# Hybrid encoder layer on one core: value products of the neighbourhood attention with the values as stationary operand, two heads on the two halves of the output partitions

## What is computed

```python
# tokens lie on a grid 64 columns wide; a query row sees 8 key rows, a block of 16 query columns sees 32 key columns
s = einsum('bhnqd,bhrnkd->bhnqrk', q_b, k_blk) + bias      # masked 2-D relative bias
p = softmax(s over the 8 x 32 keys)
o = einsum('bhnqrk,bhrnkd->bhnqd', p, v_blk)               # the value products
na = o * silu(ga)
y = x + gate * (concat(na, retention) @ w_out)
```

## Time and profile before

| | us |
|---|---|
| median of 3 runs | 3115.77 |
| profiled execution, its own time | 3119.01 |
| its span | 3117.2 |
| TensorE busy in the span | 3063.3 (98%) |
| VectorE, ScalarE, GpSimd busy | 1459.4, 862.3, 577.2 |

### The profile page before, as it was taken

The page is one execution under the profiler, slowest core; times in us unless marked ns, Lnnn a source line. Parts: engine busy times, 40 slices in busy tenths (PEclk is TensorE's granted clock), DMA queues, the critical chain, the costliest instruction groups (busy, mean ns, idle before and its releaser), DMA issues.

```text
span 3117.2 us, 49473 instructions
## 1 busy us (share of the span) xinstructions
PE 3063.3 (98%) x16480; PEld 2600.1 (83%) x16480; DVE 1459.4 (47%) x3181; ACT 862.3 (28%) x1832; POOL 577.2 (19%) x633
## 2 busy tenths in 40 slices
PE   7999999999999999999999999999999999999999
PEld 3888888888886888888888888889999988888887
DVE  4334333343334433333333333335666666777775
ACT  3232232222322211111111111125675672111111
POOL 1111111111111540000000000002333332333331
PEclk9999999999999999999999999999999999999999
DMA  7444445444446842122222212248688665555553
GB/s 281 151 143 160 147 138 167 141 137 159 144 145 250 303 136 78 72 83 80 82 77 83 83 70 79 80 154 238 185 258 251 208 202 184 202 202 202 202 202 142
DMA packets 208757, 491.04 MB, mean 158 GB/s; under 512 B 23275, under 2 KB 85739, under 8 KB 204165
## 3 DMA queue, kind: packets, MB, share of 16 engines
q1 hardware_dynamic: 199255, 462.64, 44.6%
q0 software_dynamic: 9424, 27.43, 2.7%
HBM read 306.83 MB, written 191.00 MB: 160 GB/s over the span
## 4 chain that ended last, share of the span: by engine, by line
PE 64%; issue 1%; ACT 1%; DVE 1%; DMA 1%; SPq 0%; POOL 0%; ACTq 0%; DVEq 0%
PE proj L329 27%; PE t_bank L1761 7%; PE o_bank L1512 7%; PE s_bank L1761 4%; PE o_bank L1761 4%; PE t_bank L1498 3%; PE s_bank L1488 3%; PE r_kv L1068 2%; PE s_bank L1751 1%; PE r_so L1078 1%; PE r_so L1077 1%; PE r_so L1055 1%; PE s_bank L1743 1%; PE r_qkT L1047 1%; DMA bias_table<-tables_d 1%
## 5 line engine op out<-in xcount | busy, mean ns | idle before, releaser
L329 PE MATMUL proj<-w_att_hi,a_h_hi 128*128 128x512 f32 x2560 | 1024.3, 400 | 13.1 <-DVE a_h_lo L430 7.1
L329 PE MATMUL proj<-w_att_hi,a_h_lo 128*128 128x512 f32 x2560 | 1001.9, 391 | 0.0
L329 PE MATMUL proj<-w_att_lo,a_h_hi 128*128 128x512 f32 x2560 | 1000.2, 391 | 0.0
L329 PEld LDWEIGHTS proj<-w_att_hi,a_h_hi 128*128 128x128 f32 x2560 | 483.2, 189 | 106.9 <-DVE a_h_lo L430 7.4
L329 PEld LDWEIGHTS proj<-w_att_hi,a_h_lo 128*128 128x128 f32 x2560 | 482.0, 188 | 102.9
L329 PEld LDWEIGHTS proj<-w_att_lo,a_h_hi 128*128 128x128 f32 x2560 | 483.4, 189 | 92.5
L1512 PE MATMUL o_bank<-v_strip,probs_T 120*128 120x64 f32 (+2 forms) x2112 | 278.9, 273 | 12.8 <-ACT probs_T L1353 11.1
L1512 PEld LDWEIGHTS o_bank<-v_strip,probs_T 120*128 120x128 f32 (+2 forms) x2112 | 266.3, 193 | 27.3 <-ACT probs_T L1353 16.0
L1307 POOL CAST q_block<-q_strip 128x512 fp32r<-128x512 f32 x80 | 49.6, 620 | 1270.0 <-DMA q_strip<-q_d 950.5
L1345 ACT ACTIVATE probs<-biased,neg_max 128x360 f32<-128x360 f32 (+3 forms) x320 | 218.4, 684 | 90.8 <-DVE neg_max L1400 87.9
L561 POOL TENSOR_TENSOR qk_stat<-qk_stat,minus_half 128x8 f32<-128x8 f32 x80 | 131.3, 1642 | 526.0 <-DVE qk_stat L655 526.0
(11 more groups left out here) (155 smaller groups left out, 4260.0 us busy)
## 6 DMA issues: line engine op xcount, KB each, us to landing
k_strip<-kT_d SPq DMA_DIRECT2D x12, 1920.0 KB, 11.3
a_x<-in_x SPq DMA_DIRECT2D x40, 512.0 KB, 4.4
a_xT<-in_xT SPq DMA_DIRECT2D x40, 512.0 KB, 5.2
h_d<-a_h_hi SPq DMA_DIRECT2D x40, 512.0 KB, 2.7
h_d<-a_h_lo SPq DMA_DIRECT2D x40, 512.0 KB, 3.5
kT_d<-k_parts SPq DMA_DIRECT2D x80, 256.0 KB, 3.5
q_strip<-q_d SPq DMA_DIRECT2D x40, 512.0 KB, 6.7
o_x<-in_x SPq DMA_DIRECT2D x40, 512.0 KB, 4.4
```

The lines of the kernel that those rows point to most:

```text
L329: last = self.nc.tensor.matmul(bank, h[:, par, k, :], w[:, n, k, :], start=(k == 0 and j == 0), stop=(k == KB - 1 and j == 2))
```

## The change

The value products swap operands. The values [keys x 64] of a head are stationary, the turned probabilities [keys x 128 queries] moving, and the result is transposed, [64 x 128 queries]. Heads 0 and 2 write output partitions 0 to 63, heads 1 and 3 partitions 64 to 127; the heads of a pair alternate chunk by chunk. So `o_bank` columns 0 to 255 hold the four heads' transposed results in two blocks. ScalarE copies these [128 x 256] to SBUF (`take_out_T`), TensorE turns the two blocks back (`turn_back`, two transposes with the identity, into columns 256 to 511 of the same bank), one unit later, and VectorE scales from there. `probs_T` gets a second buffer, one for each pair. TensorE's order in a unit becomes turn 0, turn 1, scores, turn 2, turn 3, value pair 0, turn back of the unit before, value pair 1.

To make room the last block of output weights moves into memory of the first k strip: it is loaded by SP's queue behind the first tile loads of the output stage and split in the last unit instead of the first edge body. The load of the output gate rows waits for the last scores. On VectorE the last two `scale_unit` calls move behind parts of the output stage's first tile. TensorE's first body stands outside its loop.

```diff
 def unit(b, u, edge, next_edge, split=False, first=False):   # ScalarE
     j = GH * u
+    if not first:
+        take_out_T(b, u - 1)
     take_out(b, j, edge)
...
+def take_out_T(b, u):
+    act.wait_ge(valued, STEPS * b + GH * (u + 1))
+    at_least(act, turned_back, UNITS * b + u - 1)
+    nc.scalar.activation(out_T[:, u % 2], o_banks[u % 2][:, 0:GW], ACT.Copy).then_inc(out_T_made, 1)
...
 def unit(b, slot, next_slot, u, edge, next_edge, first=False, split=False):   # VectorE
     take_out(b, j + 1, edge)
-    for k in range(4):
+    for k in range(3):
         add_bias(b, next_slot, j + GH + k, next_edge)
+    take_out(b, j + 3, edge)
+    add_bias(b, next_slot, j + GH + 3, next_edge)
     if not first:
         scale_unit(b, u - 1)
-    take_out(b, j + 3, edge)
...
-def value(b, j, edge, v_loads):
-    pe.wait_ge(turned_act if j % 2 == 0 else turned_dve, STEPS // 2 * b + j // 2 + 1 + T_CREDIT)
+def value(b, u, pair, edge, v_loads):
+    n = STEPS // 2 * b + 2 * u + pair + 1 + T_CREDIT
+    pe.wait_ge(turned_act, n)
+    pe.wait_ge(turned_dve, n)
...
     for c in range(chunks):
-        last = nc.tensor.matmul(o_banks[u % 2][:, cols], probs_T[0:group, j % 2, c, :],
-                                v_strip[u // COLS][0:group, slots[c], cols],
-                                start=(c == 0), stop=(c == chunks - 1))
-    last.then_inc(valued, 1)
+        for i in range(2):
+            h = 2 * pair + i
+            last = nc.tensor.matmul(o_banks[u % 2][i * NHD:(i + 1) * NHD, pair * P:(pair + 1) * P],
+                                    v_strip[u // COLS][0:group, slots[c], h * NHD:(h + 1) * NHD],
+                                    probs_T[pair][0:group, i, c, :], start=(c == 0), stop=(c == chunks - 1))
+            if c == chunks - 1:
+                last.then_inc(valued, 1)
+
+def turn_back(b, u):
+    pe.wait_ge(out_T_made, UNITS * b + u + 1)
+    for pair in range(2):
+        cols = slice(pair * P, (pair + 1) * P)
+        last = nc.tensor.transpose(o_banks[u % 2][:, GW:2 * GW][:, cols], out_T[:, u % 2, cols], ident[:])
+    last.then_inc(turned_back, 1)
...
 # the end of the stage on ScalarE and on VectorE
 o.make_decay(act)
+take_out_T(BODIES - 1, UNITS - 2)
 take_out(BODIES - 1, STEPS - GH, True)
 take_out(BODIES - 1, STEPS - GH + 2, True)
+w_out.make_hi(act, KB - 1)
 o.square(act, 0)
+take_out_T(BODIES - 1, UNITS - 1)
...
-scale_unit(BODIES - 1, UNITS - 2)
 dve.wait_ge(o.decay_made, 1)
 o.carry(dve, 0, 0, 0)
+take_out(BODIES - 1, STEPS - GH + 3, True)
+w_out.make_lo(dve, KB - 1)
 o.total_up(dve, 0, 0, 0)
-take_out(BODIES - 1, STEPS - GH + 3, True)
+scale_unit(BODIES - 1, UNITS - 2)
 o.norm(dve, 0, 0)
 o.mix_up(dve, 0, 0)
+scale_unit(BODIES - 1, UNITS - 1)
 o.carry(dve, 1, 1, 0)
-scale_unit(BODIES - 1, UNITS - 1)
```

More of the change, by code:

```diff
@@ L88 @@
 K0_AT = Q1_AT + Q_BYTES + 4 * 2 * 4 * P
+LAST_W_AT = K0_AT + 2 * 8 * D
+K1_AT = K0_AT + 4 * (GH * KR * W + V_SLOTS * GW)
 def strip_shape(column, edge):
@@ L1293, in _ @@
         o.load_first_mix(sp)
-        for half in range(2):
-            store_pass(BODIES - 1, half)
+        store_pass(BODIES - 1, 0)
+        wait_apart(sp, scored, STEPS * BODIES)
+        o.load_gate_rows(sp)
+        store_pass(BODIES - 1, 1)
     @block.gpsimd
@@ L1323, in _ @@
         body(BODIES - 4)
-        for k in range(KB // 2, KB):
+        for k in range(KB // 2, KB - 1):
             w_out.load(pool, k)
@@ L1350, in take_out, with unit @@
             act.wait_ge(probs_turned, STEPS * b + j + 1)
-            at_least(act, valued, STEPS * b + j - 1)
+            at_least(act, valued, STEPS * b + j - 3)
             _, chunks, group, _ = strip_shape(j // GH % COLS, edge)
-            nc.scalar.activation(probs_T[0:group, 0, 0:chunks].rearrange("p c q -> p (c q)"),
+            nc.scalar.activation(probs_T[j // 2 % 2][0:group, 0, 0:chunks].rearrange("p c q -> p (c q)"),
                                  t_banks[0][0:group, 0:chunks].rearrange("p c q -> p (c q)"),
                                  ACT.Copy).then_inc(turned_act, 1)
-        def unit(b, u, edge, next_edge, split=False):
+        def take_out_T(b, u):
+            act.wait_ge(valued, STEPS * b + GH * (u + 1))
+            at_least(act, turned_back, UNITS * b + u - 1)
+            nc.scalar.activation(out_T[:, u % 2], o_banks[u % 2][:, 0:GW], ACT.Copy).then_inc(out_T_made, 1)
+        def unit(b, u, edge, next_edge, split=False, first=False):
             j = GH * u
+            if not first:
+                take_out_T(b, u - 1)
             take_out(b, j, edge)
@@ L1364, in unit, with body @@
             exponentiate(b, j + GH + 3, next_edge)
-            if split:
+            if split and u < KB - 1:
                 w_out.make_hi(act, u)
-        def body(b, edge, next_edge, units=UNITS, split=False):
+        def body(b, edge, next_edge, units=UNITS, split=False, first=False):
             for u in range(units):
-                unit(b, u, edge, next_edge if u == UNITS - 1 else edge, split)
+                unit(b, u, edge, next_edge if u == UNITS - 1 else edge, split, first and u == 0)
         act.sem_inc(turned_act, T_CREDIT)
@@ L1377, in _ @@
             if g == 0:
-                body(0, False, False)
+                body(0, False, False, first=True)
             with act.Fori(b0 + (g == 0), b0 + INNER - 1) as b:
@@ L1523, in unit, with body @@
                 score(b, u + 1, next_edge)
-            else:
+            turn(b, j + 2, edge)
+            turn(b, j + 3, edge)
+            value(b, u, 0, edge, v_loads)
+            if not first:
+                turn_back(b, u - 1)
+            if last:
                 pe.wait_ge(biased_made, STEPS * BODIES)
                 o.cross(pe, 0, 0, 0)
[L1527 to L1534, removed]
+            value(b, u, 1, edge, v_loads)
+        def body(b, edge, next_edge, v_loads, first=False):
             for u in range(UNITS):
-                unit(b, u, edge, next_edge if u == UNITS - 1 else edge, v_loads,
+                unit(b, u, edge, next_edge if u == UNITS - 1 else edge, v_loads, first and u == 0,
                      isinstance(b, int) and b == BODIES - 1 and u == UNITS - 1)
@@ L1552, in _ @@
             edges = before + INNER * INNER_V_LOADS
-            with pe.Fori(b0, b0 + INNER - 1) as b:
+            if g == 0:
+                body(0, False, False, INNER_V_LOADS, first=True)
+            with pe.Fori(b0 + (g == 0), b0 + INNER - 1) as b:
                 body(b, False, False, INNER_V_LOADS * (b - b0 + 1) + before)
```

55 lines of the change are left out of this document (31 added, 24 removed).

## The result

| | before | after |
|---|---|---|
| median of 4 runs each, us | 3116.23 | 3059.31 (3055.91 to 3063.43) |
| ratio, 95% interval | | 0.9817 (0.9805 to 0.983) |
| profiled execution, us | 3119.01 | 3055.91 |
| its span | 3117.2 | 3054.1 |

What follows compares the result with a forecast made beforehand. TensorE, busy 98% of the span, was taken as the bound. Inner bodies -23, edge bodies -4, weight block -1 and the end +2 sum to -26 us, giving 3090; own range 3065 to 3108, 8 in 10 within 3045 to 3150.

Steps and rivals of the forecast that it cites:

- the value products' slots: Inner half body: n chunks of two heads take 2n + 1 slots of 0.109 us, 6.98 us, saving 5.5.
- The overlap itself: Value products: both halves of the array work at the same time; bounds 0.109 us for each pair and half of it.
- Changes of width: Four switches between full and half array per unit: 0.34 us a round trip, 2.7 us for a half body.
- The old side: Value products removed from an inner half body: 112 x 0.1116 = 12.5 us.
- Turning back: Two transposes in each unit turn the result back: 8 x 0.11 = 0.9 us for a half body.
- I count 0: Last two bodies wait for ScalarE: no gain, apart from -1 us for the weight block no longer split there.
- The end: Path to the first mix: VectorE gets the last block's split and a scale; +2 us, bounds 0 and 3.
- (b): Value products: the halves work one after another, no overlap; about 3177 us; chance 0.20.
- (a): Value products: head B's operand load waits until A's second pass has started; 3120 us, no change; chance 0.19.
- (c): Width changes cheap, loads hidden at 64 columns; transfers keep a body at 44 us or more; 3045 us; chance 0.08.
- (d): ScalarE's copy for value pair 1 comes 0.5 us late in each unit, costing 40 us; 3130 us; chance 0.10.
- The forecast's own range: Whole kernel: 3065 to 3108 us, by the bounds of the overlap and of the width changes.

Runs made afterwards that it cites:

- on one half: Changed kernel with both heads of a pair writing the same half of the output partitions: 3155.38 us (one run).
- the order alone: Changed kernel with the value products of the kernel before, keeping the new order, second buffer and moved weight block: 3111.29 us.
- turning back first: Changed kernel with the transposes that turn back ahead of value pair 0 instead of between the pairs: 3042.9 us.
- the fastest kernel: Changed kernel with turn-back transposes ahead of value pair 0 and ScalarE making a weight block's high part right behind the unit's first copy: 3034.95 us.

## Why the prediction was wrong in size

**The failed step is the value products' slots**: "the two passes of one product use the same half and must follow each other, so ... 2n + 1 slots". The first half of it is right (on one half the starts were 0.11 us apart) and the conclusion is not: it let B's first pass start only with A's second, as if one order held both halves. B's first pass starts beside A's first, so n chunks take 2n slots: 12.2 us for an inner body instead of 14.0, 1.75 less. The overlap itself, which the prediction took without a row of before, held: 6.1 us for a half body, twice as fast as on one half, where the inner body took 12.1 us more (55.5 against 43.4).

**The other terms of an inner body**, 6.6 us measured against 3.8:
- Changes of width: 0.15 + 0.15 instead of 0.145 + 0.196; for 32 changes 4.8 instead of 5.4. Going back to the full array was priced as if its whole first load lay open. That the price exists, from rows of two-column products, held, and was confirmed by taking changes away and adding them. What TensorE does in the 0.15 us is not shown.
- The old side: 25.0 was put in for the products, and 25.4 went: 0.8 of stalls, which the order alone removes, and 224 pairs at 0.110 (the old products, 49.2, less what is there now, gives 5.8 + 12.2 + 1.75 + 4.8 = 24.6).
- Turning back: 1.75 against 1.8.

1.75 + 0.6 + 0.4 + 0.05 is the 2.8 that was missed: for six inner bodies 17 of the missing 31 us. The same slots and changes make the edge bodies' 4.45 instead of 2.1 (5 us). The slots alone are 14 of the 31, the largest part.

**"I count 0" for the last bodies** was wrong by some 3 us: the seven units behind the split body were TensorE's for the most part and gained 3.1. The split body itself went as reasoned: it gained 1.2 us, no more than the 1.5 that its clock accounts for, its wait is ScalarE's, and it could be taken away on ScalarE alone.

**The end**, +2 forecast, was +0.9, of which the split of the last block is 0.2; the last turning back waits 1.0 us for its copy there.

**Rivals.** (b) No overlap: the kernel on one half is that rival, at 3155 instead of 3177, and a break-even of about 0.08 us for a pair fits (0.109 was 39 us slower than before, half of that 57 faster), but the halves do overlap. (a) fell with the starts in twos. (c) gave a floor of 44 us for a body from a busy share of 0.88; turning back first ran that body in 41.1 us at 311 GB/s and a busy share of 1.02, so the 0.88 at 277 GB/s was no bound there. The loads did bind in two profiled executions, by 13.4 and 3.6 us, but at shorter bodies than forecast. (d) came true in the edge bodies and once in the first body: TensorE's waits for that copy are 9 us in all, by the waits view of the changed kernel, not 40.

**The sum again**, as measured: 6 x 6.6 for the inner bodies, 2 x 4.45 for the edge bodies, 3.1 for the last units, less 0.9 at the end, is 50.7 us, what runs at the same clock show. The other 6 of the 57 are clock, which the prediction had no term for; why the changed kernel ran at a higher mean clock stays open. The forecast's own range, which the result missed, was narrower than the bounds that it names: half of 0.109 for each pair, with all else as forecast, is already 14 us below 3090, and free changes of width another 54.

## What to carry to other kernels

Products of 64 result rows ran fully side by side on the two halves of the array with the heads in turn chunk by chunk (inner bodies of 43.4 us, 55.5 on one half) and nearly so in runs of two (43.8), but not with one head behind the other (49.4): let the halves take turns. Each change between half and full array cost 0.15 us, so gather the narrow work: one stretch in a unit instead of two was worth 16 us here. And once TensorE's share shrinks, look at what was just hidden: a 1 us piece of ScalarE work in the wrong place was worth 9 us of one body, and a strip load was the next to bind, by 3.6 us in the fastest kernel.

## What the runs showed of the hardware

- A product on one half started ahead of products for the other half that stand before it in the program: with one head behind the other, the second head's first pass fell together with the third of six or the fifth of eight of the first.
- Runs of two products for each half cost 0.4 us of an inner body (43.8 against 43.4), runs of three or four 6.0 (49.4).
- A change of width cost 0.15 us in either direction: eight transposes took 0.87 us behind scores and 1.02 behind value products; an inner body with 16 changes fewer took 41.0 us, with 16 more 45.8, against 43.4.
- VectorE's subtraction `w_out_lo` (128 x 1024) took 2.19 us instead of 1.22 when it started during GpSimd's placing of queries; where it started first, GpSimd took 2.11 instead of 1.26.
